# Gate and up projections of three transformer blocks by seven quarter products in place of eight

## The reference, cut to what matters

```
x = x + square(relu(h @ w_up)) @ w_down                  # MLP: 1024 -> 4096 -> 1024
x = x + 0.5 * mod * ((silu(h @ w_gate) * (h @ w_up)) @ w_down)   # FFN, four times: 1024 -> 2816 -> 1024
h = rms_norm(x) * gain * (1 + scale) + shift             # scale and shift come from c @ w_ada, 72 columns of 1024
```

## Time and profile before

| | |
|---|---|
| time, median of 3 runs (lowest, highest) | 3504.78 us (3500.11, 3506.03) |
| span of the profiled execution | 3498.8 us |
| busy: PE, PEld | 3407.7, 2738.7 us |
| busy: DVE, ACT, POOL | 1179.6, 885.8, 2369.8 us |
| matrix products | 17034 |

### The profile page before, as it was taken

How to read it: one execution, slowest core, us unless ns; L and a number is a source line. 1 busy time by engine, 2 the same in 40 slices (tenths; PEclk the granted TensorE clock), 3 DMA queues, 4 the chain that set the end, 5 groups by cost and what they waited for, 6 DMA issues and landing times.

```text
span 3498.8 us, 42521 instructions
## 1 busy us (share of the span) xinstructions
PE 3407.7 (97%) x17034; PEld 2738.7 (78%) x17034; DVE 1179.6 (34%) x2514; ACT 885.8 (25%) x1876; POOL 2369.8 (68%) x1242
## 2 busy tenths in 40 slices
PE   8888999999999999999999999999999999999999
PEld 6655777988898888667779888888887677798887
DVE  6554332433443234442223111332244422241111
ACT  2656551211120102354312000210012543221000
POOL 7515447787778776645677877687775546678775
PEclk9999999999999999999999999999999999999999
DMA  3222213444535442212232222254432122223222
GB/s 142 68 69 82 67 62 108 149 171 170 185 127 204 168 166 94 73 58 85 85 106 96 97 97 96 83 220 165 171 126 73 67 76 79 82 97 106 98 98 73
DMA packets 104773, 388.09 MB, mean 111 GB/s; under 512 B 12017, under 2 KB 12401, under 8 KB 98433
## 3 DMA queue, kind: packets, MB, share of 16 engines
q1 hardware_dynamic: 88272, 292.76, 24.4%
q10 hardware_dynamic: 16304, 92.62, 7.0%
HBM read 383.20 MB, written 2.13 MB: 110 GB/s over the span
## 4 chain that ended last, share of the span: by engine, by line
PE 92%; DVE 4%; ACT 3%; issue 1%; ACTq 0%; DVEq 0%
PE psum L1234 28%; PE psum L1236 27%; PE psum L1235 27%; PE psum L1307 2%; PE psum L1349 2%; PE psum L1324 2%; PE psum L1293 1%; DVE rs_t L1695 1%; ACT s_sb L1477 0%; DVE s_sb L1736 0%; ACT L1477 0%; ACT s_sb L1495 0%; PE psum L1407 0%; PE psum L1285 0%; DVE n_sum L1906 0%
## 5 line engine op out<-in xcount | busy, mean ns | idle before, releaser
L1202 POOL TENSOR_TENSOR w_hi<-raw,ones 128x1024 fp32r<-128x1024 f32 (+2 forms) x593 | 1041.3, 1756 | 990.4 <-PE psum L1236 981.2
L1205 POOL TENSOR_TENSOR w_lo<-raw,w_hi 128x1024 fp32r<-128x1024 f32 (+2 forms) x593 | 1315.1, 2218 | 46.5
L1234 PE MATMUL psum<-h_hi,w_hi 128*128 128x512 f32 (+2 forms) x2912 | 1143.4, 393 | 19.4 <-DVE r L1711 9.4
L1236 PE MATMUL psum<-h_hi,w_lo 128*128 128x512 f32 (+2 forms) x2912 | 1105.3, 380 | 0.0
L1235 PE MATMUL psum<-h_lo,w_hi 128*128 128x512 f32 (+2 forms) x2912 | 1104.8, 379 | 0.0
L1234 PEld LDWEIGHTS psum<-h_hi,w_hi 128*128 128x128 f32 (+1 forms) x2912 | 550.2, 189 | 156.6 <-issue 35.9
L1236 PEld LDWEIGHTS psum<-h_hi,w_lo 128*128 128x128 f32 (+1 forms) x2912 | 549.7, 189 | 106.6
L1235 PEld LDWEIGHTS psum<-h_lo,w_hi 128*128 128x128 f32 (+1 forms) x2912 | 550.9, 189 | 103.3 <-issue 9.0
L1234 PE MATMUL psum<-a_hi,w_hi 128*128 128x512 f32 (+1 forms) x1064 | 392.5, 369 | 0.0
L1235 PE MATMUL psum<-a_lo,w_hi 128*128 128x512 f32 (+1 forms) x1064 | 391.8, 368 | 0.0
L1236 PE MATMUL psum<-a_hi,w_lo 128*128 128x512 f32 (+1 forms) x1064 | 391.8, 368 | 0.0
(11 more groups left out here) (198 smaller groups left out, 3299.5 us busy)
## 6 DMA issues: line engine op xcount, KB each, us to landing
raw<-weights_dram SPq DMA_DIRECT2D x487, 512.0 KB, 3.3
ada_t<-ada_dram ACTq DMA_DIRECT2D x48, 1536.0 KB, 7.1
raw<-weights_dram SPq DMA_DIRECT2D x76, 256.0 KB, 2.6
raw<-weights_dram SPq DMA_DIRECT2D x32, 384.0 KB, 2.9
bias_t<-biases_dram ACTq DMA_DIRECT2D x36, 256.0 KB, 2.9
bias_t<-cum_dram ACTq DMA_DIRECT2D x16, 256.0 KB, 3.9
out_dram<-x SPq DMA_DIRECT2D x8, 256.0 KB, 2.1
raw<-weights_dram SPq DMA_DIRECT2D x4, 408.0 KB, 3.1
```

What stands on the lines that cost most here:

```text
L1202: nc.gpsimd.tensor_tensor(high, piece, ones[:, 0:1].to_broadcast([P, n]), ALU.mult)\
L1205: nc.gpsimd.tensor_tensor(w_lo[:, p % NR, 0:n], piece, high.bitcast(F32), ALU.subtract)\
L1234: mm(dst, lh, rh, start=first, stop=False)
L1236: return mm(dst, ll, rh, start=False, stop=last)
```

## The change

Two chunks of 128 output columns and 8 input tiles make a "pair". A pair is cut into quarters of the weights (a, b of the first chunk, c, d of the second: 512 inputs by 128 outputs) and quarters of h (512 inputs by 256 tokens). Before, a pair was 8 quarter products. It is now 7 (P1 to P7), of sums of quarters, each 12 matrix products of 256 columns, and their results are added up afterwards. A "set" is two pairs, gate and up (in the MLP, four up chunks), whose products alternate: P1, P1, P2, P2, P5, P5, P6, P6, P7, P7, P3, P3, P4, P4.

What is new around them: `move` (ACT copies c to PSUM banks 0 and 1), `first_sums` and `next_sum` (DVE makes c+a, then +d, +a, +b, the four sums S3, S1, S2, S4), `high_of` (ACT makes all 7 high parts of a pair), `low_of` (POOL makes the low parts of P1, P2, P7, P4, and DVE those of P5, P6, P3), `keep` (ACT copies P1, P5 and P6 out of PSUM), `combine` (DVE adds them back, c22 and c1), and `quarter_sum`, `sums_low` and `sums_high`, which make the four sums of quarters of h, t_hi and t_lo, 1024 columns for each k of 0 to 3, once behind each of the five norms. The norm's tile is now `n_out` in SBUF instead of a PSUM bank. Four groups instead of three run by halves behind a norm; they keep the old form, so that 47 sets are left: 7 in the MLP, 10 in each FFN. A part of the MLP has two sets (the first only one), the parts of an FFN 3, 4 and 3. The sums of `ada_t` are 72 of 1 MB, all in down parts (10, 9 or 6 in one). Each product has a place in the ring of 6 that pieces had; its operands are made when the place 6 before is free. The diff, cut to its core:

```diff
 NR = 8
 NH = 6
 GATES = 24
-ADA = 3
+ADA = 2
...
+def quarter_sums(m):
+    m.sums = TOTAL.get("t_lo", 0)
+    for k in range(KC // 2):
+        assert tick("t_sum") == tick("t_hi") == m.sums + k + 1
+        put("tsum", m, k)
+        yield k
+        if k:
+            put("tlow", m, k - 1, tick("t_lo"))
+    put("tlow", m, KC // 2 - 1, tick("t_lo"))
...
             next(second)
+    sums = quarter_sums(m) if m.quartered else iter(())
     for c in range(KC):
         for g in firsts:
             mm(g, c, c + 1, 1)
-        next(second, None)
+        if next(second, None) is None:
+            next(sums, None)
+    for _ in sums:
+        pass
...
+BY = dict(P1=("act", "pool"), P2=("act", "pool"), P5=("act", "dve"), P6=("act", "dve"), P7=("act", "pool"),
+          P3=("act", "dve"), P4=("act", "pool"))
...
+    for what in PRODUCTS:
+        for p in pairs:
+            p.ops[what].done = tick("product_done")
+            put("product", p.ops[what])
+            if what == "P1":
+                p.p1 = tick("copied")
+                put("keep", p, "P1")
+            elif what == "P5":
+                p.p5 = tick("copied")
+                put("keep", p, "P5")
+            elif what == "P6":
+                p.u2 = tick("copied")
+                put("keep", p, "P6")
+            elif what == "P7":
+                p.c22 = tick("combined")
+                put("c22", p)
+            elif what == "P3":
+                p.c1 = tick("combined")
+                put("c1", p)
+                result(p, 0)
+            elif what == "P4":
+                result(p, 1)
...
+            one = RING[place]
+            needed = [one] if isinstance(one, int) else one.pair.pieces
+            if any(p >= NR and p - NR not in gone for p in needed):
...
-        if step[0] == "mask":
-            yield step
+        if step[0] in ("prep", "mm", "product"):
+            yield from ready()
+        yield step
         if step[0] == "mm" and step[3] == step[1].n and step[1].ends_piece and (step[1].half > 0 or step[5]):
-            used += len(step[1].pieces)
-            yield from ready()
+            for p in step[1].pieces:
+                gone.add(p)
...
+            def product(op):
+                pair, what, m = op.pair, op.what, op.pair.norm
+                E.wait_at(op.low)
+                if what == "P1":
+                    E.wait_at(pair.before[1])
+                    E.wait_ge("h_lo", m.scales[KC - 1, 1][0])
+                elif what == "P2":
+                    E.wait_at(pair.before[0])
+                elif what == "P6":
+                    E.wait_ge("copied", pair.p1)
+                elif what == "P7":
+                    E.wait_ge("copied", pair.u2)
+                elif what == "P4":
+                    E.wait_ge("combined", pair.c22)
+                elif what == "P3":
+                    E.wait_ge("copied", pair.p5)
+                which, right = dict(P2=(0, 0), P5=(0, 1), P3=(0, 1)).get(what, (1, 0))
+                dst = half_bank(pair, which, right)
+                wh, wl = high_of(op), low_of(op)
+                for k in range(KC // 2):
+                    if what in ("P1", "P2", "P3"):
+                        c, cs = k + KC // 2 * (what != "P1"), columns(int(what == "P3"))
+                        hi, lo = h_hi[:, c, cs], h_lo[:, c, cs]
+                    else:
+                        E.wait_ge("t_lo", m.sums + k + 1)
+                        j = dict(P5=0, P6=1, P7=2, P4=3)[what]
+                        hi, lo = t_hi[:, k, j, :], t_lo[:, k, j, :]
+                    w = slice(k * P, (k + 1) * P)
+                    start, stop = k == 0 and what in ("P1", "P2", "P5"), k == KC // 2 - 1
+                    mm(dst, wh[:, w], hi, start=start, stop=False, skip_group_check=True)
+                    mm(dst, wh[:, w], lo, start=False, stop=False, skip_group_check=True)
+                    ins = mm(dst, wl[:, w], hi, start=False, stop=stop, skip_group_check=True)
+                ins.then_inc(sem["product_done"], 1)
             def norm_sum(m, half):
...
+            def move(pair):
+                E.wait_at(pair.sums_before)
+                E.wait_at(loaded(pair.pieces[1]))
+                fn(sums(pair), quarters(pair)[2], ACT.Copy).then_inc(sem["moved"], 1)
+            def operand(op):
+                gate, up = SETS[op.pair.made // 8]
+                if (op.what, op.pair) == ("P2", up):
+                    move(gate)
+                elif (op.what, op.pair) == ("P5", gate):
+                    move(up)
+                if op.high[0] != "high_act":
+                    return
+                if op.place >= NH:
+                    E.wait_at(freed(op.place))
+                src, ready = source_of(op)
+                E.wait_at(ready)
+                fn(high_of(op), src, ACT.Copy).then_inc(sem["high_act"], 1)
+            def keep(pair, what):
+                if pair.former:
+                    E.wait_ge("combined", pair.former.c22 if what == "P5" else pair.former.c1)
+                E.wait_ge("product_done", pair.ops[what].done)
+                if what == "P5":
+                    src, dst = half_bank(pair, 0, 1), kept_5[:, pair.side, :]
+                else:
+                    src, dst = half_bank(pair, 1, 0), kept[:, pair.side, columns(int(what == "P6"))]
+                fn(dst, src, ACT.Copy).then_inc(sem["copied"], 1)
...
+            def quarter_sum(m, k):
...
+                    E.wait_ge("t_lo", m.sums + k - 1)
+                v.tensor_tensor(t[0], n_out[:, k, far], n_out[:, k, near], ALU.subtract)\
+                    .then_inc(sem["dve_chain"], 1)
+                E.settle()
+                v.scalar_tensor_tensor(t[1], n_out[:, c, far], shift[:, c:c + 1], t[0], ALU.add, ALU.subtract)\
+                    .then_inc(sem["dve_chain"], 1)
+                v.scalar_tensor_tensor(t[2], n_out[:, k, far], apart[:, k:k + 1], n_out[:, c, far], ALU.subtract,
+                                       ALU.subtract).then_inc(sem["dve_chain"], 1)
+                E.n += 1
+                E.settle()
+                v.scalar_tensor_tensor(t[3], n_out[:, c, near], shift[:, c:c + 1], t[1], ALU.add, ALU.subtract)\
+                    .then_inc(sem["t_sum"], 1)
...
+            def sums_low(m, k):
+                E.wait_ge("t_hi", m.sums + k + 1)
+                v.scalar_tensor_tensor(t_lo[:, k, :, :], t_new[:, k % 2, :, :], -1.0, t_hi[:, k, :, :].bitcast(F32),
+                                       ALU.mult, ALU.subtract).then_inc(sem["t_lo"], 1)
+            def first_sums(pair):
+                a, _, c, d = quarters(pair)
+                E.wait_at(loaded(pair.pieces[0]))
+                E.wait_ge("moved", pair.moved)
+                v.tensor_tensor(c, sums(pair), a, ALU.add).then_inc(sem["sums_made"], 1)
+                E.wait_at(summed(pair, "S3"))
+                v.tensor_tensor(sums(pair), sums(pair), d, ALU.add).then_inc(sem["sums_made"], 1)
+            def next_sum(pair, what):
+                a, b, _, _ = quarters(pair)
+                E.wait_at(pair.ops["P5" if what == "S2" else "P6"].low)
+                v.tensor_tensor(sums(pair), sums(pair), a if what == "S2" else b, ALU.add).then_inc(sem["sums_made"], 1)
+            def combine(pair, what):
+                if what == "c22":
+                    E.wait_ge("product_done", pair.ops["P7"].done)
+                    E.wait_ge("copied", pair.p5)
+                    v.tensor_tensor(half_bank(pair, 1, 1), half_bank(pair, 1, 0), kept_5[:, pair.side, :], ALU.add)\
+                        .then_inc(sem["combined"], 1)
+                else:
+                    E.wait_ge("product_done", pair.ops["P3"].done)
+                    E.wait_ge("copied", pair.u2)
+                    v.tensor_tensor(bank(pair.banks[0]), bank(pair.banks[0]), kept[:, pair.side, :], ALU.add)\
+                        .then_inc(sem["combined"], 1)
+            def operand(op):
+                gate, up = SETS[op.pair.made // 8]
+                if (op.what, op.pair) == ("P2", up):
+                    first_sums(gate)
+                elif (op.what, op.pair) == ("P5", gate):
+                    first_sums(up)
+                if op.low[0] == "low_dve":
+                    E.wait_at(op.high)
+                    v.tensor_tensor(low_of(op), sums(op.pair), high_of(op).bitcast(F32), ALU.subtract)\
+                        .then_inc(sem["low_dve"], 1)
+                if op.what in ("P5", "P6"):
+                    next_sum(op.pair, "S2" if op.what == "P5" else "S4")
```

More of the change, by code:

```diff
@@ L62 @@
 PIECES = []
-SPLITS = []
+RING = []
+SETS = []
 HELD = {}
@@ L93 @@
     split: int
+    used: int
+    n: int = 0
+    pair: object = None
+    second: bool = False
 def new_piece(key, cols, split=True):
-    PIECES.append(Piece(key, cols, len(SPLITS) if split else -1))
+    PIECES.append(Piece(key, cols, len(RING) if split else -1, sum(not p.pair for p in PIECES)))
     if split:
-        SPLITS.append(len(PIECES) - 1)
+        PIECES[-1].n = tick("w_hi")
```

(58 more changed lines are left out.)

307 lines of the change are left out of this document (226 added, 81 removed).

## The result

The changed kernel takes 3581.22 us (median; 3572.99 to 3584.53) against 3502.61 us of the kernel before on the same chip: ratio 1.022, 95% interval 1.0204 to 1.0235. It is slower by 2.2%. The profiled execution has a span of 3571.2 us, 72.4 us more than before.

A forecast was written before the change was run, and what follows sets the result against it. PE was taken to bound the kernel, busy 97%. Savings of 75.2 us against added costs summed to +18.8 us; on the median of 3504.78 that gave 3523 us predicted, range 3472 to 3568.

The forecast's parts named there:

- The saving on PE: On PE, a set falls from 21.76 to 20.16 us; 1.60 us for each of 47 sets, -75.2 us.
- Rival C: On PE, a short product takes half the time of a long one: 128 us saved, 3471 us; chance 0.03.
- Sets of an FFN: Within a set and between two sets of an FFN nothing waits, with 0.35 us left: 0 us.
- rival D: The FFN's sets wait for each other, 1.35 us at each of 28 places: 3561.6 us; chance 0.20.
- FFN starts: At the beginning of an FFN, DVE's order delays t_lo and P5: +7.0 us, four times, 28 in all.
- MLP start: At the beginning of the MLP, the same delay with four evacuations instead of two in front: +10.8 us.
- set to set: Between two sets of the MLP, four evacuations stand among the sums: +4.0 us, three times, +12.
- rival B: The beginnings hide, the sums of h costing PE nothing: 3431 to 3451, say 3440 us; chance 0.07.
- h_lo in the closing halves: In closing stretches, h_lo with two SBUF inputs can lose up to a POOL split: +3 us for each of 5 norms, +15.
- rival A: Only the order's own waits; no h_lo clash with POOL, no clock fall, ada_t sums hide: 3489.6 us; chance 0.24.
- Loads of ada_t: In down parts, fourth and fifth xadd of an MLP part late, 2 us in each of 3 parts: +6 us.
- The clock: Behind stalls at five beginnings and three MLP places, PE's clock falls: 1.6 us each, +13 us.

The follow-up runs named there:

- Run 4: Changed kernel with all four sums of h and t_lo ahead of the first groups' evacuation in DVE's and ACT's order: 3555.39 us, ratio 1.0154 to the kernel before.
- run 6: Changed kernel with the first half of the norm's tile in PSUM again in closing parts, copied to n_out by ACT: 3561.75 us, ratio 1.0175 to the kernel before.
- run 3: Changed kernel with the MLP's up projection in its old form, whole chunks, FFNs as changed: 3546.29 us, ratio 1.0119 to the kernel before.
- run 2: Changed kernel without the ada_t loads behind the first two of each block, sums kept but reading old data: 3536.9 us, ratio 1.01 to the kernel before.
- run 9: Changed kernel with the small instructions behind the ada_t sums on POOL, same place in the order: 3576.84 us, ratio 1.0205 to the kernel before.
- run 10: Changed kernel with old-form MLP up projection, ada_t and h sums reordered, norm's first half in PSUM, small instructions on POOL: 3467.86 us, ratio 0.9903 to the kernel before.
- run 5: Changed kernel with the eight small DVE instructions moved from a down part to behind the closing part's first down group: 3591.76 us, ratio 1.0258 to the kernel before.

## Why the prediction was wrong, by its own steps

The forecast was 3523 us, the range up to 3568; 3581 lies above. The direction was right, the sum 58 us short of the median (54 of the span: 18.8 forecast, 72.4 measured). Two terms, the loads and the clock, were far too low; the waits of the new products were 20 us too high and hid part of it.

- **The saving on PE, -75.2:** right. Products start 0.120 us apart, a set takes 20.17 us. Rival C is out.
- **Sets of an FFN, 0:** right, and the rival D is out. All of PE's waits for low parts (10.5 and 1.2 us) lie in the MLP, so in none of the 28 places of the FFNs does PE wait. How much of the 0.35 us of slack is left is not shown.
- **FFN starts, 28; MLP start, 10.8; set to set, 12; up to down, 7.6:** mechanism right, sizes somewhat high. PE idles 5.4 us at an FFN's start (four: 21.7) and 8.4 at the MLP's. Between sets it is 3.4, 2.3 and 2.9 us, together 8.6. Ahead of the down groups it is 1.36 us four times, 5.4. Run 4 shows the order on DVE as the cause for the first two. So the beginnings don't hide, and rival B is out.
- **h_lo in the closing halves, 15:** mechanism right, and rival A out. PE has gaps of 2.3 us in four of five closings, 9.2 in all, and the clock behind them; taking one input out of SBUF gave 19 us (run 6).
- **Loads of ada_t, 6:** this step failed. The idle time of PE at xadds outside the closings is 28.7 us in the MLP and some 5 us each in two FFNs, 39 us in all; with its clock the arrangement costs some 42 us in the MLP alone (run 3). Three things were wrong in it. The load of 1 MB was put at 5.2 us by an estimate from the earlier trace rows, while it measured 6.7 in the median, and with the wait behind it two buffers gave a sum every 4.8 us (734.80, 739.88, 744.69, 748.72, 754.47, 758.71), not every 3.8; ten of them take longer than a down part. I let DVE hold back xadds for 2 us in a part without following the chain past the fifth group. And I did not list the small instructions as moved, which now stand in the middle of a down part, 8.1 us of DVE. The three were separated in part: without the loads 22 of the 42 us come back in the MLP, and a gap of 8.5 us stays at the small instructions (run 2).
- **The clock, 13:** this step failed too, and follows in good part from the one before. It measures some 35 us, half of the 69 us more that PE worked at the lower clock. I counted eight stalls at 1.6 us; from the MLP's norm on PE has 30 gaps of over 1.8 us where it had 4 before. At the 2.3 us gap of a closing part stand 3.4 us at half clock (in the MLP's closing 6.8), at the two gaps of an FFN's start 6.8, and the 13.7 us at the longest gap begin 2.8 us into it. Some gaps cost no clock: PE's gap of 2.59 us that ends at 843.10 lies in a stretch at full clock:

```profile
840.00:860.00 20.00, 15.30 (x65) 11.67 (x64) 12.26 (x20) 0.63 (x1) 12.10 (x6) 1.00 0.86 309
```

Run 4 shows that fewer stalls bring clock back too (idle time 13 us less, time at half clock 44 us less, span 24.5 us less). What it takes of one gap to lower the clock was not tried by itself.

With 39 and 48 in place of 6 and 13, and the other terms as measured, the sum is -73.6 + 21.7 + 8.4 + 8.6 + 5.4 + 9.2 + 39 + 48 = 66.7 us; the other 5.7 us of the 72.4 are smaller gaps that I did not assign. The 48 is what the books leave over, so the sum has to close up to such gaps; only some 35 of it are clock.

## What to carry to other kernels

A part of a change that only makes room for the rest (here the loads of 1 MB squeezed into the down parts) is to be priced like the rest: divide the transfers by the buffers, and compare the pace with the time of the stretch, part by part. Put a price on clock beside the stalls that are forecast, for here it was some 35 us beside 98 of idle time. Two waits that lie over each other hide one another's cost: run 9 took away a gap of 11.54 us, waits for loads filled its place, and next to nothing was gained. So remove the larger one first and measure again. And an edit that undoes an earlier edit's harm (run 10 after run 5) is to be measured against the kernel without either.
